# Reordering the delta-rule block of a two-block model with a mixture of experts: gate piece, value heads, substitution and inverse in another order

## The reference

```python
proj = rms_norm_2(h, norm_g) @ w_in
f_in, qkv, z, ab, gate_f, gate_d = split(proj)
y_f = real(fft2(f_in)) @ w_fourier
q, k, v = split(silu(depthwise_conv_centred(qkv, conv_w)))
q, k = l2_normalize(q) * 128 ** -0.5, l2_normalize(k)
...
a_mat = strict_lower((k * beta) @ k.T * decay)      # 64 x 64, each chunk and head
t_mat = triangular_solve(eye + a_mat, eye)
u, w = t_mat @ (v * beta), t_mat @ (k * beta * exp(g))
...
state, o = scan(step, u, w, q, k)                   # forwards and backwards
y_d = (rms_norm_2(o) * silu(z)) @ w_delta
merged = sigmoid(gate_f) * y_f + sigmoid(gate_d) * y_d
h = h + merged @ w_out
h = h + experts(h)                                  # 64 experts, the best two of a group
```

## Time and profile before

| what | us |
|---|---|
| median of 3 runs | 1165.42 (1165.01 to 1166.71) |
| profiled execution, its own time | 1165.79 |
| its span | 1164.0 |
| TensorE busy | 1015.5 (87%) |
| VectorE busy | 508.6 (44%) |
| ScalarE busy | 380.5 (33%) |
| POOL busy | 427.6 (37%) |

### The profile page before, as it was taken

One profiled execution on the slowest core, in us unless ns is written; L12 is line 12 of the kernel. 1 busy time (PEld: TensorE's weight loads), 2 busy tenths in 40 slices (PEclk: granted clock), 3 DMA queues, 4 the chain that ended last, 5 costly groups with the idle time before them and its releaser, 6 DMA issues.

```text
span 1164.0 us, 20100 instructions
## 1 busy us (share of the span) xinstructions
PE 1015.5 (87%) x8121; PEld 799.3 (69%) x8121; DVE 508.6 (44%) x979; ACT 380.5 (33%) x572; POOL 427.6 (37%) x192
## 2 busy tenths in 40 slices
PE   9999999999999998899989899977667676676687
PEld 7999999999999998798989798433223232333232
DVE  4356965601136887768864634222222222222213
ACT  5554353444447556335343344100000000000002
POOL 5767868888876856333031271000000000000000
PEclk8999999999999999999999899988888888888889
DMA  7645546566656545115211789999999999999995
GB/s 247 212 134 151 178 128 183 179 183 186 188 172 212 150 124 162 56 54 218 81 66 37 311 284 409 379 426 428 427 428 427 428 428 428 429 427 429 426 424 230
DMA packets 43569, 304.75 MB, mean 262 GB/s; under 512 B 5092, under 2 KB 5476, under 8 KB 30952
## 3 DMA queue, kind: packets, MB, share of 16 engines
q1 hardware_dynamic: 43208, 303.21, 69.2%
q10 hardware_dynamic: 288, 0.52, 0.1%
HBM read 302.67 MB, written 1.05 MB: 261 GB/s over the span
## 4 chain that ended last, share of the span: by engine, by line
PE 51%; DMA 26%; DVE 14%; issue 3%; POOL 2%; ACT 2%; SPq 2%; DVEq 0%; ACTq 0%; POOLq 0%
DMA arena<-gate_up 24%; PE bank L486 10%; PE bank L487 9%; PE bank L488 9%; PE bank L1363 7%; PE bank L871 3%; PE bank L1384 3%; DVE arena L2352 2%; POOL rounded L2975 1%; DMA weights<-front 1%; DVE arena L2099 1%; POOL rounded L2934 1%; DVE arena L2551 1%; DVE arena L2549 1%; DMA arena<-down 1%
## 5 line engine op out<-in xcount | busy, mean ns | idle before, releaser
L2934 POOL TENSOR_TENSOR rounded<-weights,rounded 128x1024 fp32r<-128x1024 f32 x152 | 370.4, 2464 | 160.3 <-ACT rounded L1449 150.5
L486 PE MATMUL bank<-rounded 128*128 128x256 f32 (+2 forms) x776 | 219.7, 283 | 2.3 <-POOL rounded L2934 2.3
L487 PE MATMUL bank<-rounded 128*128 128x256 f32 (+2 forms) x776 | 217.1, 280 | 0.0
L488 PE MATMUL bank<-rounded 128*128 128x256 f32 (+2 forms) x776 | 216.7, 279 | 0.0
L1449 ACT ACTIVATE rounded<-weights 128x1024 fp32r<-128x1024 f32 x146 | 147.4, 1052 | 81.0 <-PE bank L488 49.4
L486 PE MATMUL bank<-rounded,rounded 128*128 128x256 f32 (+3 forms) x552 | 159.1, 288 | 3.7 <-DVEq L2354 1.6
L487 PE MATMUL bank<-rounded,rounded 128*128 128x256 f32 (+3 forms) x552 | 156.7, 284 | 0.0
L488 PE MATMUL bank<-rounded,rounded 128*128 128x256 f32 (+3 forms) x552 | 156.5, 284 | 0.0
L486 PEld LDWEIGHTS bank<-rounded 128*128 128x128 f32 (+1 forms) x776 | 145.7, 188 | 4.4 <-POOL rounded L2934 3.0
L487 PEld LDWEIGHTS bank<-rounded 128*128 128x128 f32 (+1 forms) x776 | 145.7, 188 | 0.7 <-issue 0.7
L488 PEld LDWEIGHTS bank<-rounded 128*128 128x128 f32 (+1 forms) x776 | 145.4, 187 | 0.0
(11 more groups left out here) (467 smaller groups left out, 1445.1 us busy)
## 6 DMA issues: line engine op xcount, KB each, us to landing
weights<-front SPq DMA_DIRECT2D x165, 512.0 KB, 4.2
arena<-down SPq DMA_DIRECT2D x31, 2048.0 KB, 21.6
weights<-gate_up SPq DMA_DIRECT2D x28, 2048.0 KB, 34.3
arena<-gate_up SPq DMA_DIRECT2D x28, 2048.0 KB, 33.3
weights<-front SPq DMA_DIRECT2D x4, 2048.0 KB, 8.1
weights<-gate_up SPq DMA_DIRECT2D x8, 768.0 KB, 13.2
arena<-gate_up SPq DMA_DIRECT2D x4, 1536.0 KB, 33.3
weights<-gate_up SPq DMA_DIRECT2D x4, 512.0 KB, 6.2
```

The lines of the kernel that those rows point to most:

```text
L486: nc.tensor.matmul(out, a[0], b[1], start=start, stop=False)
L487: nc.tensor.matmul(out, a[0], b[0], start=False, stop=False)
L488: return nc.tensor.matmul(out, a[1], b[0], start=False, stop=stop)
L2934: nc.gpsimd.tensor_tensor(lo, raw[q % RAW], hi.bitcast(f32), ALU.subtract).then_inc(sem("w_lo"), 1)
```

## The change

In the projections (TensorE) the gate piece `gf(2)` comes directly behind the key norm, before the first key spread; value heads 4 to 7 come one at a time between the key work. In VectorE's list the convolutions of value heads 4 to 7 spread out accordingly. The second half of the Fourier gate's weights and that of the values, two blocks before, are stored as two mixed blocks: a half of one beside a half of the other. The number of transfers stays.

The substitution begins early. Its first ten steps and the pairs addition move ahead of the query heads' convolutions, among the gated Fourier pieces and the meta solves; the rest keeps its place between the query norms. The third `unit_queries` moves behind the inverse. The inverse's buffer gets a place of its own, at the end of the arena, which POOL clears at the program's start. The transfer that used the place, `load_down_first(1, 1)`, now waits for the inverse. In the stages behind the inverse, `gd_part(1)` and `gd_part(2)` each move one stage later.

The diff, cut to its core:

```diff
 in pe():
             norms("nk", sq_k, LEN, ("sqn", 1, 2))
             turn[WK] += 1
-            for h in (4, 5): one_head("v", h, V1)
+            gf(2)
             spread("k", 0, 1, LEN)
-            for h in (6, 7): one_head("v", h, V1)
+            late_head(4)
             to_tokens("v", 0, lambda h: v_T[0][:, h, :], 1)
+            late_head(5)
             spread("k", 1, 1, LEN)
             turn[WK] += 2
-            gf(2)
+            late_head(6)
             pe.wait_ge(sem("k_done"), 2)
             meta_keys()
             pe.wait_ge(sem("gl"), 3)
             unit(0)
+            late_head(7)
             fourier_features()
...
+            pe.wait_ge(sem("yf_split"), 2)
+            wf(0)
             to_tokens("v", 1, lambda h: v_T[1][:, h, :], 2, ((6,), (7,), (3,)))
             turn[WK] += 3
-            pe.wait_ge(sem("yf_split"), 2)
-            wf(0)
             meta_level(1)
...
             gd_part(0)
-            gd_part(1)
             pe.wait_ge(sem("inverse"), 2)
             for stage in (products_32, inverses_64, products_64, inverses_128):
                 for part in range(2):
                     stage(part)
                 if stage is products_32:
+                    gd_part(1)
+                if stage is inverses_64:
                     gd_part(2)
 in dve():
             factors("nk", LEN, rn2_r, 1.0, "ssn", "sdn", 1)
+            normalize("k", 0, kT[:, 0:4], LEN, 1.0)
             for h in range(2):
                 conv(f"v{h + 4}", v_T[1][:, h, :], "v", 20 + h)
-            normalize("k", 0, kT[:, 0:4], LEN, 1.0)
-            for h in range(2, 4):
-                conv(f"v{h + 4}", v_T[1][:, h, :], "v", 20 + h)
             normalize("k", 1, kT[:, 4:8], LEN, 1.0)
+            conv("v6", v_T[1][:, 2, :], "v", 22)
...
             turn_lanes(0)
+            turn_lanes(1)
             fourier_gated(0)
             meta_t(1)
+            turn_lanes(2)
             fourier_gated(1)
-            turn_lanes(1)
+            turn_lanes(3)
+            link(nc.vector.tensor_tensor(pairs, turned, turned.rearrange("p c r -> p r c"), ALU.add))
+            dve.wait_ge(sem("cleared"), 1)
+            substitute(0, 4)
             fourier_gated(2)
             meta_t(2)
-            turn_lanes(2)
+            substitute(4, 7)
             fourier_gated(3)
-            turn_lanes(3)
+            substitute(7, 10)
             meta_t(3)
...
-            substitute(0, 8)
+            substitute(10, 14)
             normalize("q", 0, qT[:, 0:4], SEQ, P ** -0.5)
-            substitute(8, 11)
+            substitute(14, 17)
             normalize("q", 1, qT[:, 4:8], SEQ, P ** -0.5)
-            substitute(11, 13)
+            substitute(17, 19)
             unit_queries(0)
-            substitute(13, 18)
+            substitute(19, 24)
             unit_queries(1)
-            substitute(18, 23)
-            unit_queries(2)
-            substitute(23, 31)
+            substitute(24, 31)
...
+            unit_queries(2)
             unit_queries(3)
 in pool():
+            nc.gpsimd.memset(whole(inv), 0.0).then_inc(sem("pool_chain"), 1)
...
             WS_HALVES = 10
             trail(range(WS_HALVES))
...
             nc.gpsimd.tensor_tensor(hn, hn_hi_r.bitcast(f32), hn_lo_r.bitcast(f32), ALU.add).then_inc(sem("hn"), 1)
-            nc.gpsimd.memset(whole(inv), 0.0).then_inc(sem("pool_chain"), 1)
...
 in sp():
-                if ZB + i == GD:
-                    load_down_first(1, 1)
...
             load_part(1)
+            sp.wait_ge(sem("inverse"), 2)
+            load_down_first(1, 1)
             sp.wait_ge(sem("o_b"), 4)
```

41 lines of the change are left out of this document (26 added, 15 removed).

## The result

The changed kernel takes 1171.88 us in the median of 8 runs (1169.76 to 1175.62), against 1166.62 us for the kernel before in 8 runs: a ratio of 1.0039, with a 95% interval of 1.0023 to 1.0056, some 4.5 us slower (the two medians stand 5.3 us apart). Timed again later it came to 1.0045 (1.0027 to 1.0062).

The account below looks back on a forecast made before the run. Engines bound the part where the second block is computed, then DMA streaming expert weights; shifts up to step_keys count fully. 1.5 + 0.85 + 3.6 - 2.2 = +3.75 us gives 1169.5 profiled, 1169.2 against the median; range 1161.8 to 1173.0.

Parts of the forecast that it names:

- the likeliest case: VectorE's early substitution collides with GpSimd's split of query weights and decides the time: 1167 to 1171.5 us, chance 0.44.
- The one-to-one count: Any shift up to the first recurrence step (step_keys), behind the inverse, goes one to one to the program's end.
- B': Early substitution beside GpSimd's two-piece split, from about 509 us: at most one VectorE instruction stalls per piece, +3.6 us.
- A: Gate piece, value heads and key units, 440 to 473 us: changed TensorE waits, +1.5 us (ends 0.7 and 2.4).
- B: Early substitution, 497 to 520 us: 8.45 us of added VectorE work against 7.6 idle, +0.85 us.
- C: The inverse, 580 to 605 us: fewer late steps and moved gate-d parts gain time, -2.2 us.
- R2: Faster: collision misses, keys' part at its lower end, issue stall behind the products covered; about 1163.1 us, chance 0.23.
- R1: The collision misses, as GpSimd's pieces fall where VectorE reads banks or idles: +0.2, about 1165.6 us, chance 0.25.
- R3: The clock: TensorE waits over 2.5 us at the last meta level, query heads start slower; about 1172.6 us, chance 0.08.

Follow-up runs that it names:

- the third keys' order: Changed kernel with value head 4 ahead of the first key spread, second key group's norm before head 5's convolution, head 6's convolution behind the first unit's rows: 1168.13 us, 1.0002.
- the kernel with the full hold: Changed kernel with GpSimd's split of the weights of query heads 4 and 5 held until the last meta solve is done: 1167.34 us, 0.9994.
- the two kernels with the split fully held: Changed kernel with GpSimd's split held until the last meta solve, 1167.34 us (0.9994); the same with the keys' part as before the change, 1167.39 us (1.0006).
- the second pair: The kernel before and the changed kernel, both unedited, profiled and timed again: 1167.72 us (1.0004) and 1173.28 us (1.0045).
- the last kernel: Changed kernel with keys' part as before, only steps 0 to 5 early, split held until the last solve, `unit_queries(2)` ahead of the inverse: 1164.41 us, 0.9976.

## Why the prediction was right, point by point

The time, 1171.88, lies in the range and on the side forecast, 2.7 us above the 1169.2 named and 0.4 above the 1167 to 1171.5 that the likeliest case had by itself. Of the 2.7, 1.2 lie in the kernel before: its median over 8 runs is 1166.62, and the forecast started from 1165.42 over 3. The likeliest case came true: the collision is there, near the place and the size forecast, and taking it away takes the loss away. That it alone decides is not shown, since the third keys' order does the same with the collision left in. The range is wide, 1161.8 to 1173.0, and the terms below miss by up to 1.9 us each in both directions, so that the sum comes so near is in part luck.

- **The one-to-one count**: right. Step_keys 4.04 us later, span 4.0.
- **B', the collision**: the forecast was +3.6, ends 0 and 4.4. The two long instructions cost 2.26 + 2.28 - 0.19 - 0.22 = 4.1 more than in the kernel with the full hold, and the stretch shrinks by 4.2 when the split is held away. The sentence that one instruction stalls per piece is borne out. The timing behind it isn't: the pieces were to come about 2 us earlier and came 2.3 us later (from the event of the table, 70.1 instead of 67.8 us), and VectorE's early work came later as well; in all four profiles without a hold they met. And I had not seen that a meta solve could stall as well, its last instruction being of the same kind. The rule of the Trainium skill (SBUF — State Buffer, section Who interferes with whom) taken strictly gave 4.4; the measured 4.1 is nearer to that than my 3.6.
- **A, the keys' part**: +1.5 forecast. Between the two kernels with the split fully held, one with the keys as before and one not, the first query convolution moves by 80.12 - 78.36 = 1.8 us: near the forecast, but with 1 to 2 us of accident in it, for the two executions differ in their stretches at 0.50 (one of 6.8 us at 460 in the one, 3.4 at 463 and 6.8 at 490 in the other), the first transposes stand 3.5 us apart and step_keys 0.5. The further stall at 460.63 us was not counted. And the step "I expect the same again, and count nothing" for the clock failed: in four of five profiles with the changed keys' order a stretch at 0.50 of 3.4 or 6.8 us stands behind the first spread, worth 1.7 or 3.4 (an estimate, half its length), and their first transposes come 1.0 to 3.1 us later than in the fifth; with head 4 ahead of the spread it is absent. In the two profiles of the kernel before it is absent, although the wait there is 2.65 to 2.7; of six other kernels with the old order, two have it.
- **B, the early steps**: +0.85 forecast, ends 0 and 1.7; measured 78.36 - 75.65 = 2.7. The working has a slip: four switches at 0.25 are 1.0 us and not the 0.5 that stands in its sum, which makes 8.95 us and +1.35. The failing step is that the added work fills all of 7.6 us idle time. The first hole can't be filled by them (1.85 us are left), and the pairs addition has its own 2.0 to 2.07 us where the estimate from two additions of 512 took 1.25.
- **C, the inverse**: -2.2 forecast, ends 0 and 3.9; measured from z_part(0) to step_keys, 61.40 before and 57.68 after: -3.7. (The lower end of the gain was 604.39 - 603.1 = 1.3, not 1.4.) The step that failed is "the stall is TensorE's own issue", from which I took the smaller half: with a gate-d part between the stages the stall isn't there in any of the ten kernels that have it there (0.6 us of issue at most). That part of R2 came true.

The sum at step_keys, 166.40 - 160.40 = 6.0, is then 1.8 (A) + 1.7 (the clock behind the spread) + 2.7 (B) + 4.1 (B') - 3.7 (C) - 0.4 (from the query convolution to z_part(0)), 6.2 in all, against +3.75 forecast; two terms that were too small and one clock that was left out against one gain that was too small. It is the sum of one pair of profiles: the second pair gives 167.96 - 164.35 = 3.6, and the medians 4.5 to 5.3 lie between. Of the profiled difference 2 us are hidden by the clock at 9.4 us. So step_keys at 608.43, "near 608" as forecast, is luck; the first query convolution (527.71, not 523 to 526) and the first product (593.5, not 590 to 592) came later than the signs named.

**R1** (the collision misses) is what the kernel with the full hold shows: forecast 1165.6, measured 1167.34 at a ratio of 0.9994, so even without the collision the change gains nothing. **R2** needs that, the keys as before and a shorter stretch of early steps, which the last kernel shows: 2.8 us less than the kernel before, where R2 had 2.35. **R3** (the low clock at the query heads): its signs came too, a wait of 5.9 us at the meta level and a stretch of 6.8 us at 0.50 from 518 us on, but that overlaps time in which VectorE is the bound, and the 6.8 us at 491 us are gone in exchange; what it costs by itself was not measured.

## What to carry to other kernels

Work that is moved into an engine's idle time must be checked against what the other engine does in its new place: a few tiny instructions with both operands in SBUF, 0.2 us each, cost 4 us beside GpSimd's long ones, and holding GpSimd back by one wait gave the whole loss back. A loss that one edit gives back can still have a second cause: another order of the keys gave it back as well. Move no more than the holes really take, hole by hole: six steps were free, ten delayed the path by 2.7 us. Two moves that show no gain one by one, an earlier result and work moved behind its user, gave 2.8 us together: each alone leaves TensorE standing, 4.1 us for the result or 1.7 us behind the products.

## What was not expected of the hardware

- The waiting goes both ways: where the pairs addition had started ahead of GpSimd's first piece, the two pieces took 5.58 to 5.63 us instead of 4.75, in three profiles. Where the addition had just ended, at the start of the piece, they took 4.74.
- The granted clock falls to 0.50 for stretches of about 3.4 or 6.8 us, at different places in executions of the same program: at 9.4 us in one profile of the kernel before, at 81 us in the other, and in the changed kernel behind the same wait of 3.0 us for 3.4 us in one profile and for 6.8 in the other. In the kernel with the split fully held, the wait is 3.0 too, and the clock behind it stays full:

```profile
443.20:450.00 6.80, 5.51 (x45) 5.43 (x46) 4.34 (x11) 6.23 (x10) 4.47 (x2) 1.00 0.17 42
```

Each such stretch is worth up to 1.7 or 3.4 us (an estimate, half its length, where TensorE is the bound). The twelve runs of one kernel lie 4 to 8 us apart; how much of that these stretches make is not shown, since one run of each has a trace. What decides where they fall, these runs don't show.
- The stall of about 2 us that the profile gives as issue, behind the 32x32 products, comes when products follow directly on each other there (1.95 before, 1.7 with six early steps alone) and not when a gate-d part lies between. Its cause wasn't tried.
